# Query weights of seven heads copied within DRAM, packed by head, before they are loaded: a two-layer encoder on one core

## What is computed

```python
def peer_ffn(h, w_q, sub_keys, u, v):
    b, s, d = h.shape
    t = b * s
    x = h.reshape(t, d)
    q = (x @ w_q).reshape(t, PEER_HEADS, 2, PEER_D_HALF)
    scores = jnp.einsum('thcd,cnd->thcn', q, sub_keys).astype(jnp.float32)
    top_s, top_i = lax.top_k(scores, PEER_TOPK)
    ...
```

## Time and profile before

| | |
|---|---|
| Median of 3 runs | 3493.96 us (3489.74 to 3494.89) |
| The profiled execution, own time | 3489.76 us |
| Its span, first to last instruction | 3487.9 us |
| PE busy | 2807.9 us, 81% |
| DVE busy | 2079.6 us, 60% |
| POOL busy | 1360.6 us, 39% |
| ACT busy | 900.7 us, 26% |
| DMA, mean rate over the span | 384 GB/s |

### The profile page before, as it was taken

The page is one execution under the profiler, slowest core; times in us unless marked ns, Lnnn a source line. Parts: engine busy times, 40 slices in busy tenths (PEclk is TensorE's granted clock), DMA queues, the critical chain, the costliest instruction groups (busy, mean ns, idle before and its releaser), DMA issues.

```text
span 3487.9 us, 26775 instructions
## 1 busy us (share of the span) xinstructions
PE 2807.9 (81%) x7404; PEld 1300.4 (37%) x7404; DVE 2079.6 (60%) x3766; ACT 900.7 (26%) x2304; POOL 1360.6 (39%) x1046
## 2 busy tenths in 40 slices
PE   7889967776778888888888788998888866766776
PEld 6444434443324333333333333443433322222222
DVE  4562677666677455545564755545555567777675
ACT  4341122221222123224121322332422222222221
POOL 4000355665555222223242522222234255555554
PEclk9999989999989999999999999999999988888888
DMA  4423899999999999999999999999999999999998
GB/s 145 158 99 121 337 414 416 416 415 410 421 407 420 417 417 417 417 417 419 417 410 418 406 417 417 417 417 417 417 416 408 418 413 419 421 419 418 414 419 356
DMA packets 239510, 1339.10 MB, mean 384 GB/s; under 512 B 27089, under 2 KB 48145, under 8 KB 105745
## 3 DMA queue, kind: packets, MB, share of 16 engines
q0 software_dynamic: 147456, 1073.81, 74.4%
q1 hardware_dynamic: 91920, 263.73, 19.6%
HBM read 1335.36 MB, written 2.10 MB: 383 GB/s over the span
## 4 chain that ended last, share of the span: by engine, by line
DMA 66%; PE 20%; DVE 6%; issue 5%; POOL 2%; ACT 1%; DVEq 0%; ACTq 0%; SPq 0%; POOLq 0%
DMA room<-in_peer_v_dram,index 62%; PE psum L1123 11%; DMA room<-in_peer_u_dram,index 4%; PE psum L989 2%; PE psum L1177 1%; PE psum L934 1%; POOL room L711 1%; PE psum L1013 1%; PE psum L750 1%; DVE resid L2155 1%; POOL room L723 1%; DVE room L2143 0%; PE psum L794 0%; PE psum L768 0%; PE psum L796 0%
## 5 line engine op out<-in xcount | busy, mean ns | idle before, releaser
L1123 PE MATMUL psum<-room,diag 128*128 128x512 f32 x3008 | 1573.3, 664 | 629.7 <-DMA room<-in_peer_v_dram,index 596.4
L2143 DVE CUSTOM_DVE_ANT_0 room<-room,normed 128x2048 f32<-128x2048 f32 x512 | 1172.8, 2291 | 659.7 <-DMA room<-in_peer_u_dram,index 651.8
L1123 PEld LDWEIGHTS psum<-room,diag 128*128 128x128 f32 x3008 | 584.4, 207 | 1545.6 <-issue 1256.6
L723 POOL DMA_INDIRECT room<-in_peer_v_dram,index x512 | 744.0, 1453 | 1033.7 <-PE psum L1123 992.3
L711 POOL DMA_INDIRECT room<-in_peer_u_dram,index x512 | 575.2, 1123 | 1041.8 <-DVE dots L2143 577.9
L1177 PE MATMUL psum<-wbuf,normedT 128*128 128x512 f32 x1536 | 694.2, 595 | 0.0
L1531 ACT ACTIVATE acts<-dots 128x1 f32<-128x1 f32 x512 | 103.6, 202 | 1827.2 <-DVE dots L2143 1826.8
L2155 DVE SCALAR_TENSOR_TENSOR resid<-room,acts,resid 128x512 f32<-128x512 f32 (+1 forms) x512 | 401.7, 785 | 285.2 <-DMA room<-in_peer_v_dram,index 284.9
L1177 PEld LDWEIGHTS psum<-wbuf,normedT 128*128 128x128 f32 x1536 | 284.6, 190 | 328.7 <-issue 325.6
L1540 ACT ACTIVATE diag<-ident,acts 128x128 f32<-128x128 f32 x512 | 205.5, 401 | 49.4 <-ACT acts L1535 2.6
L1535 ACT ACTIVATE acts<-acts,gates 128x1 f32<-128x1 f32 x512 | 150.9, 295 | 16.7
(11 more groups left out here) (224 smaller groups left out, 1687.4 us busy)
## 6 DMA issues: line engine op xcount, KB each, us to landing
wbuf<-in_fox_w_in_dram SPq DMA_DIRECT2D x128, 1024.0 KB
wbuf<-in_fox_w_o_dram SPq DMA_DIRECT2D x32, 1024.0 KB
wbuf<-in_peer_w_q_dram SPq DMA_DIRECT2D x32, 1024.0 KB
wbuf<-in_peer_w_q_dram SPq DMA_DIRECT2D x32, 512.0 KB, 12.0
wbuf<-in_mla_w_in_dram SPq DMA_DIRECT2D x8, 1024.0 KB, 7.2
wbuf<-in_mla_w_kvb_dram SPq DMA_DIRECT2D x32, 256.0 KB, 3.5
room<-in_mla_w_o_dram SPq DMA_DIRECT2D x8, 1024.0 KB, 11.8
room<-in_peer_u_dram,index POOLq DMA_INDIRECT x512
```

The source lines that it names most:

```text
L723: pool.indirect_dma_start(v_ring[:, r, :], None, v_table, bass.IndirectOffsetOnAxis(index[:, number % 2, s:s + 1], 0)).then_inc(v_full[r], 16)
L1123: mm = pe.matmul(psum[:, q, :], diag[:, r, :], v_ring[:, r, q * TILE:(q + 1) * TILE], start=at == 0 or n == SOLO and q == PE_BANKS - 1, st ...
L2143: V.tensor_tensor_reduce(u_ring[:, r, :], u_ring[:, r, :], normed[:, b, :], 1.0, 0.0, ALU.mult, ALU.add, dots[:, r:r + 1]).then_inc(dot_do ...
```

## The change

A DRAM tensor of 7 x 128 x 4096 values is added. ACT, after `copy_kv(0)` and ahead of its loop over groups, issues seven DMAs. Each copies one head's 2 MB from the rows of `w_q` (128 x 16 pieces of 1 KB) to the new tensor, where the 16 KB of a partition lie together. SP waits for all seven ahead of head 1's load, and then loads each head with two DMAs, each of 128 pieces of 8 KB, where it had four DMAs of 512 pieces of 1 KB. The counts that PE waits for follow. Head 0 is loaded as before.

```diff
+        laid_q = nc.dram_tensor("laid_q", (PHEADS - 1, P, KC * 2 * P), F32, kind="Internal").ap()
...
+        q_laid = sem("q_laid")
...
+        def pq_loaded(h):
+
+            return 32 * (h // PQ_TILES + 1) + (32 if h % PQ_TILES == 0 else 0)
...
-                for q in range(4):
-                    sp.dma_start(pq_tile[:, r, 4 * q:4 * q + 4, :],
-                                 w[:, 4 * q:4 * q + 4, h * 2 * P:(h + 1) * 2 * P]).then_inc(pq_full[r], 16)
+                if h == 1:
+                    sp.wait_ge(q_laid, 16 * (PHEADS - 1))
+                for half in range(2):
+                    sp.dma_start(pq_tile[:, r, 8 * half:8 * half + 8, :].rearrange("p k n -> p (k n)"),
+                                 laid_q[h - 1][:, half * D:(half + 1) * D]).then_inc(pq_full[r], 16)
...
-                    pe.wait_ge(pq_full[r], 64 * (h // PQ_TILES + 1))
+                    pe.wait_ge(pq_full[r], pq_loaded(h))
...
                 copy_q(0)
                 copy_kv(0)
+                w = rows_view(peer_w_q[0])
+                for h in range(1, PHEADS):
+                    act.dma_start(laid_q[h - 1].rearrange("p (k n) -> p k n", k=KC),
+                                  w[:, :, h * 2 * P:(h + 1) * 2 * P]).then_inc(q_laid, 16)
                 with act.Fori(0, mla.groups - 1) as g:
                     both_transposed(g)
                     copy_q(g + 1)
                     attention(mla, g)
                     copy_kv(g + 1)
```

## The result

The changed kernel takes 3528.56 us (median of 5 runs, 3527.35 to 3532.39) against 3493.47 us for the kernel before (5 runs): a ratio of 1.0103, 95% interval 1.0088 to 1.0118. The profiled execution took 3528.56 us, span 3526.7.

The account below looks back on a forecast made before the run. The prediction took DMA to bound the slots, and hand-offs among PE, ACT and DVE the first mixer. 54 + 7.5 + 1 - 7 = +55.5 us on 3493.96 gave 3549, range 3516 to 3578.

Parts of the forecast that it names:

- The hold follows the packets queued ahead: ACT after copy_kv(0): the seventh copy issue returns once 11,100 packets have moved, about 1,200 left; 54 us held.
- The price of a packet from DRAM to DRAM: Copies on ACT's queue: 77.8 ns per packet of 1 KB, between bounds of 48.3 and 97 ns.
- SP's loads in the hold: While ACT is held, SP's 3.1 MB of w_kvb and group 1 loads share the DMA engines: 7.5 us.
- The restart: PE's clock when it restarts after standing still during ACT's hold: 1 us (0 to 3).
- The gain of the wide loads: Loading heads 1 to 7 in rows of 8 KB instead of 1 KB saves 7 us, ends 6 and 8.
- Edits costed at nothing: SP's fewer issues and wait for q_laid, sooner weights, slowed gathers and group 2's loads: each counted as nothing.
- The issues don't hold ACT: ACT's queue takes all seven copies at 0.45 us each, adding 3.2 us; total time 3490 us; chance 0.15.
- The hold is short: ACT is held, but copies overlap read and write: +25 to +35 us, 3519 to 3529; chance 0.15.
- The signs: In changed profile: L1440 near 165 us, DMA near full 104 to 180 us, later issues held 8 to 10 us.

## Why the prediction was right, and which term was off

The direction, the place and the mechanism were right, and 3528.56 lies in the range of 3516 to 3578. The forecast of 3549 was 20 us too high, from one term.

- *The hold follows the packets queued ahead.* Right. 11,100 packets were to be moved before ACT is let go; 11,289 were. The doubled copies and the copies in 8 KB pieces confirm it. The limit read from SP's queue holds for ACT's, as a size: 1,200 was predicted, and 1,000 packets were left ahead of the last issue in the changed kernel, 1,114 with 8 KB pieces, 1,360 with the copies doubled and 1,450 behind the mixer. It isn't one fixed number: the changed kernel's second issue came back at 105.0 us with 1,700 packets left ahead of it, the third with 1,640. What sets the count within 1,000 to 1,700 no run shows.
- *The price of a packet from DRAM to DRAM.* This term was mis-sized. I had the bounds 48.3 and 97 ns and took 77.8 between them, because no stretch moved over 421 GB/s to or from HBM. Measured are 52.2 ns in the changed kernel and 52.9 alone. The 421 GB/s is what the 16 engines moved when gathers filled them; it was no limit of the memory, which served 628 GB/s of reads and writes in the doubled run. A copied packet cost nearly what a loaded one of the same 1 KB did, 48.3 ns, so writing it added 4 to 5 ns to reading it and not another 48. 11,100 x (77.8 - 52.2) / 16 = 17.8 us of the 20 are this term.
- *SP's loads in the hold.* 7.5 us; q1's share of 17.8% of 45 us is 8.0. Right.
- *The restart.* 1 us was counted. The granted clock was 0.86 from 147 to 167 us, after PE had stood still for 42.6 us, where the kernel before has 1.00 in the same stretch, and its first group of four matmuls took 2.77 us in place of 1.46; but ACT's table load came 43.7 us late and the mixer's last load 43.1, so nothing was lost in that execution. With the copies alone and with the copies doubled 1.7 and 1.6 us were (42.4 and 44.1, 89.5 and 91.1); with the copies alone the second group of four matmuls, too, took 3.50 us, where it took 1.98 in the changed kernel. The range of 0 to 3 holds.
- *The gain of the wide loads.* 7 us; 6.8 measured alone (ratio 0.9979), and 42.9 - 35.1 = 7.8 as the difference of the two kernels with copies. The measured packet prices were the right ones.
- *Edits costed at nothing.* SP's wait for `q_laid` and the restart of SP's loads: right.
- *The rivals.* "The issues don't hold ACT" is out: it had 3.2 us for the seven. "The hold is short" came true: it gave 3519 to 3529 with the reason that read and write overlap, and 3528.56 lies at its upper end. So the forecast holds by its range and its mechanism, while its middle rested on a limit that isn't there. The rival had 0.15 and deserved more, since the loads' own rows of 1 KB were the nearest.
- *The signs.* L1440's successor was to start near 165 us and starts at 148.43 (its table load at 147.13). The DMA engines were to be near full to 180 us and are so to about 160. From the mixer's last load to the end the kernel was to be 7 us shorter and is 4.3 in the two profiled executions. Each later issue was to be held 8 to 10 us, where the six are held 2.2, 13.7, 6.1, 7.9, 6.2 and 7.6. The hold of 44.4 us lies 10 under the 54 to 62 that the prediction gave as its test, and by the measured sizes it comes out: 11,289 packets at 52.2 ns are 36.8 us, and SP's 8.0 make 44.8. The bytes written grew by 14.68 MB, as foreseen.

## What to carry to other kernels

In this kernel an issue behind a burst on ACT's queue came back only when 1,000 to 1,700 packets were left ahead of it, and SP's queue showed about the same size (1,200). The hold went by packets: 44.4 us for 14,336 of them, 12.7 for the same bytes in 1,792. So multiply pieces by DMAs before putting a burst on an engine that others wait for. Ask what the queue stands in front of, and spread the issues so that one is drained before the next: seven copies at once cost 43 us, the same seven one per group nothing that can be told from noise, and the change then pays (-5.8 us from ACT, -6.5 from POOL). POOL, which wasn't held, flooded the DMA engines instead, and PE waited 20.1 us for `w_qb`; so look also for the loads with no slack at that time.

## What the runs showed of the hardware that I had not expected

- A copy from DRAM to DRAM in pieces of 1 KB ran at 314 GB/s each way, 52.9 ns a packet, where a load of such pieces took 48.3.
- POOL's queue took the 14,336 pieces of seven copies in 8.16 us, where ACT's was held 44. The page of that run counts 3,696 packets more on POOL's queue for the 14.68 MB (151,152 against 147,456), which are 3,584 packets of 4 KB and 112 small ones. So a packet of the profile isn't always one contiguous piece: by this count four pieces of 1 KB of the source went into one. ACT's queue shows 14,448 for the same copies, one for each piece and the 112. Whether this is why POOL isn't held, no run shows. The landings weren't sooner: a median of 31.9 us, where ACT's have 20.8, though POOL's were all issued within 8 us and so stand in line longer.
- Two queues with work moved packets in equal number in two stretches, though their sizes differed. In the kernel before, from 430 to 440 us, SP's 1 KB loads and the gathers of 8 KB moved the same number; with the copies in 8 KB pieces, from 114 to 118 us, ACT's 8 KB and SP's smaller pieces did:

```profile
q0 software_dynamic: 497, 3.60, 87.5%
q1 hardware_dynamic: 497, 0.50, 14.9%
...
q10 hardware_dynamic: 143, 1.17, 77.0%
q1 hardware_dynamic: 145, 0.26, 25.0%
```

- So large pieces on one queue slowed small ones on another here. Beside copies in 8 KB pieces, four loads of 192 KB in pieces of 1.5 KB took 21.1 us to land, against a median of 3.3 before. The four of `w_kvb` issued at the start of the copies took 15.4 us beside pieces of 8 KB and 6.7 beside pieces of 1 KB.
